# Output-projection products between the units of a dilated attention stage, and two expert weight loads held behind a gather

## The reference

```
proj = rmsnorm(x) @ w_in                      # 4992 columns, split among three head groups
mix  = [hgrn readout (384) | differential attention readout (384) | dilated attention (256)]
h    = x + mix @ w_out                        # 1024 x 1024
u    = rmsnorm(h);  logits = u @ router       # 4 groups, 16 experts; top group, top 2 inside
h    = h + sum over experts of gate * (silu(u @ wg) * (u @ wu)) @ wd
y    = norm(h + sigmoid(rmsnorm(h) @ w_gate) * (p @ w_proj))
```

## Time and profile before

| | |
|---|---|
| three runs | 1004.59, 1002.18, 995.37 us; median 1002.18 |
| profiled execution, first to last instruction | 1003.8 us |
| PE busy | 911.3 us, 91% |
| DVE, ACT, POOL busy | 381.7, 238.8, 82.6 us |
| mean granted TensorE clock | 0.948 of full |
| bytes through DMA | 209.55 MB, mean 209 GB/s |

### The profile page before, as it was taken

The page is one execution under the profiler, slowest core; times in us unless marked ns, Lnnn a source line. Parts: engine busy times, 40 slices in busy tenths (PEclk is TensorE's granted clock), DMA queues, the critical chain, the costliest instruction groups (busy, mean ns, idle before and its releaser), DMA issues.

```text
span 1003.8 us, 15625 instructions
## 1 busy us (share of the span) xinstructions
PE 911.3 (91%) x6377; PEld 483.7 (48%) x6377; DVE 381.7 (38%) x804; ACT 238.8 (24%) x600; POOL 82.6 (8%) x96
## 2 busy tenths in 40 slices
PE   6996999999999999979878993899999898898996
PEld 4453555655456876655445552344344343243442
DVE  5107455564226666454553126311121111111463
ACT  4125222220223323453313111100001000003344
POOL 1000000000024443000000000100000000002100
PEclk9998999999999999967889996899999999999998
DMA  6836133035347753244603707799999999995111
GB/s 220 309 152 178 34 147 147 1 147 183 147 138 235 240 176 109 74 162 144 196 22 122 293 23 281 290 371 372 405 395 383 392 397 410 402 338 187 44 42 44
DMA packets 71186, 209.55 MB, mean 209 GB/s; under 512 B 19113, under 2 KB 51332, under 8 KB 62540
## 3 DMA queue, kind: packets, MB, share of 16 engines
q1 hardware_dynamic: 56432, 185.53, 50.3%
q0 software_dynamic: 3936, 14.22, 4.3%
q10 hardware_dynamic: 10748, 8.80, 2.8%
HBM read 189.09 MB, written 38.26 MB: 226 GB/s over the span
## 4 chain that ended last, share of the span: by engine, by line
PE 78%; DMA 9%; DVE 7%; ACT 4%; issue 2%; SPq 0%; ACTq 0%; DVEq 0%; POOLq 0%
PE ps L2015 17%; PE ps L2427 10%; PE ps L2020 10%; PE ps L2320 6%; PE ps L2550 6%; PE ps L2464 5%; DMA EXPERT<-in_moe_w_up 4%; DMA aF<-in_moe_w_up 2%; PE ps L2052 2%; PE ps L2389 2%; PE ps L2423 2%; PE ps L2098 2%; PE ps L2179 2%; PE ps L2026 1%; PE ps L2125 1%
## 5 line engine op out<-in xcount | busy, mean ns | idle before, releaser
L2015 PE MATMUL ps<-xT,EXPERT 128*128 128x512 f32 x384 | 175.8, 603 | 0.5 <-DVE xT L1310 0.5
L2020 PE MATMUL ps<-EXPERT,xT 128*128 128x384 f32 (+1 forms) x384 | 119.0, 451 | 1.6 <-ACT EXPERT L974 1.6
L2015 PEld LDWEIGHTS ps<-xT,EXPERT 128*128 128x128 f32 x384 | 70.1, 192 | 75.3 <-issue 72.4
L2020 PEld LDWEIGHTS ps<-EXPERT,xT 128*128 128x128 f32 x384 | 77.5, 236 | 23.6 <-issue 1.8
L1917 DVE TENSOR_TENSOR dF<-dF,ps 64x512 f32<-64x512 f32 (+1 forms) x24 | 14.4, 601 | 163.5 <-ACT dF L1206 163.5
L2427 PE MATMUL ps<-EXPERT,wk 128*32 128x512 f32 x448 | 55.6, 642 | 7.8 <-DMA EXPERT<-in_moe_w_up 7.3
L2320 PE MATMUL ps<-EXPERT,xT 128*128 128x512 f32 x128 | 57.2, 597 | 1.1 <-ACT xT L1142 1.1
L2427 PE MATMUL ps<-EXPERT,samp 128*32 128x512 f32 x384 | 57.8, 594 | 0.0
L2550 PE MATMUL ps<-EXPERT 128*128 128x512 f32 x128 | 56.0, 594 | 1.3 <-DVE EXPERT L1970 1.3
L1210 ACT ACTIVATE dF<-ps 128x256 f32<-128x256 f32 (+1 forms) x24 | 8.4, 348 | 166.4 <-PE ps L2447 163.6
L1488 DVE TENSOR_REDUCE small<-ps 128x2 f32<-128x256 f32 (+3 forms) x24 | 19.8, 824 | 63.9 <-PE ps L2101 63.9
(11 more groups left out here) (472 smaller groups left out, 1319.2 us busy)
## 6 DMA issues: line engine op xcount, KB each, us to landing
EXPERT<-in_moe_w_gate SPq DMA_DIRECT2D x12, 2048.0 KB, 17.9
EXPERT<-in_moe_w_up SPq DMA_DIRECT2D x12, 2048.0 KB, 14.5
EXPERT<-in_moe_w_down SPq DMA_DIRECT2D x12, 2048.0 KB, 19.4
EXPERT<-in_w_in SPq DMA_DIRECT2D x13, 1536.0 KB, 6.7
out_win_sample<-in_cache_win SPq DMA_DIRECT2D x16, 1022.0 KB
aF<-in_cache_k_diff SPq DMA_DIRECT2D x32, 192.0 KB, 2.5
aF<-in_cache_v_diff SPq DMA_DIRECT2D x32, 192.0 KB, 2.5
Yd<-wk ACTq DMA_DIRECT2D x34, 128.0 KB
```

What stands on the lines that cost most here:

```text
L2015: last = t.matmul(ps[:, u % 2, :], W_[:, c, c0:c0 + w], xT[:, c, 0:SEQ], start=(c == 0), stop=(c == DC - 1))
L2020: last = t.matmul(ps[:, u % 2, 0:w], rows_, W_[:, c, c0:c0 + w], start=(c == 0), stop=(c == DC - 1))
```

## The change

**Order and gate.** Slab 3 is projected before slabs 10 and 12. The gate's activation and gain and the readout of tile 0 (now in three steps, `roa` on DVE, `roe` on ACT, `rob` on DVE) stand between the last differential units.

**Dilated stage.** `dilated_steps` writes the whole stage out by hand: for unit k it issues `c_s(k)`, `c_t(k-1)`, the steps of `first[k]`, `c_pv(k-1)`, the steps of `second[k]`. Scores have one pair of banks (2 and 3), so `c_s(n)` waits for the exponentials of unit n - 1. Banks 4 and 5 go in turns (`bank_turns`, semaphores `filled` and `taken`) to the transposes of a tile's 768 readout columns (`mtp`, copied to `mixT` by ACT), to the products with row blocks 0 to 5 (`wop`, which DVE adds to the reloaded rows of `XM`), and, once a tile's dilated columns are merged into `mixD`, to their transposes (`mtd`, into `dcols`) and the products with blocks 6 and 7 (`wof`). The sample rows keep one product (`wos`). Root mean square, unit rows, columns and logits of the tiles stand at the end of the list, in the order tile 0, 1, 2, sample, 3. The last `krows` and the routing's constants (`constants`) move between the units too.

**Queues.** SP loads `w_out` in three parts, reloads each tile's input rows right after `mtp` (between the `cached` loads), and writes the values of the differential attention earlier. The expert weights of step 1 now also wait for the last `c_pv`; those of step 0 for the last `wof`; the first two blocks of step 2 wait for the landing of the first gather. The stores to `u2d` move from SP's queue to POOL's, behind its own constants and ahead of its gathers.

```
-ORDER = (0, 1, 2, 4, 5, 6, 7, 9, 11, 8, 10, 12, 3)
+ORDER = (0, 1, 2, 4, 5, 6, 7, 9, 11, 8, 3, 10, 12)
...
+        if u == last[units[u][1]] and c1 == DC and at == NSLAB - 2:
+            steps.append(("w_out_load", 1))
...
+    gated = [("gate_fn",), ("gate_mul",), ("roa", 0), ("roe", 0), ("rob", 0)]
+    at_gate = None
...
+        if at_gate is None and (not todo or todo[0][0] > max(last[3], summed[3])):
+            at_gate = k
+        if at_gate is not None and gated and k >= at_gate:
+            steps.append(gated.pop(0))
+            at_gate = k + GATE_LAG
...
+    steps += gated + [("w_out_load", 0), ("outputs",)]
...
+def dilated_steps():
+    first = {
+        0: mixed_columns(0),
+        1: [("wop", 0, 0, 0), ("wop", 0, 0, 1), ("roa", 1)],
+        2: [("wop", 0, 1, 0), ("wop", 0, 1, 1)],
+        3: mixed_columns(1) + [("roa", 2)],
+        4: [("wop", 1, 0, 1), ("wop", 1, 1, 0)],
+        5: [("wop", 1, 1, 1)],
+        6: [("wop", 2, 0, 0), ("wop", 2, 0, 1), ("roa", 3)],
+        7: [("wop", 2, 1, 0), ("wop", 2, 1, 1)],
+        8: mixed_columns(3) + [("w_out_load", 2)],
+        9: [("wop", 3, 0, 1), ("wop", 3, 1, 0)],
+        10: [("wop", 3, 1, 1)],
+        11: [("mtd", 0)],
+        12: [("wof", 0, 0), ("wof", 0, 1)],
+        13: [("mtd", 1), ("rms", 0)],
+        14: [("wof", 1, 1)],
+        15: [("mtd", 2), ("rms", 1)],
+        16: [("col", 0), ("wof", 2, 1)],
+    }
+    second = {
+        0: [("dec_soft",), ("krows", 0)],
+        1: [("dec_norm",), ("krows", 1), ("krows", 2), ("roe", 1)],
+        2: [("rob", 1), ("krows", 3), ("dec_wt",)],
+        3: values(0) + [("roe", 2), ("wop", 1, 0, 0)],
+        4: values(1) + [("rob", 2)],
+        5: mixed_columns(2) + values(2),
+        6: values(3) + [("roe", 3)],
+        7: values(4) + [("rob", 3)],
+        8: values(5) + [("wop", 3, 0, 0)],
+        9: values(6),
+        10: values(7),
+        11: [("dec_out",)],
+        12: [("roa", NT), ("krows", KR_EARLY), ("roe", NT)],
+        13: [("rob", NT), ("wof", 1, 0), ("krows", KR_EARLY + 1), ("krows", KR_EARLY + 2)],
+        14: [("krows", KR_EARLY + 3), ("krows", KR_EARLY + 4), ("mt",), ("reload", NT), ("constants",)],
+        15: [("wof", 2, 0)],
+        16: [("wos",), ("log", 0), ("rms", 2), ("urow", 0), ("mtd", 3), ("col", 1), ("wof", 3, 0), ("log", 1), ("wof", 3, 1),
+             ("rms", 3), ("urow", 1), ("col", 2), ("log", 2), ("urow", 2), ("col", 3), ("rms", 4), ("log", 3), ("col", 4),
+             ("urow", 3), ("urow", 4), ("log", 4)],
+    }
+    steps = []
+    n_units = 4 * NT
+    for k in range(n_units + 1):
+        if k < n_units:
+            steps.append(("c_s", k))
+        if k:
+            steps.append(("c_t", k - 1))
+        steps += first[k]
+        if k:
+            steps.append(("c_pv", k - 1))
+        steps += second[k]
+    return steps
...
+            def reload(i):
+                src = a["x_prompt"][0, i * P:(i + 1) * P, :] if i < NT else a["x_sample"].rearrange("b t d -> (b t) d")
+                if i < NT:
+                    sp.wait_ge(filled[5], after(("mtp", i, 1)))
+                else:
+                    sp.wait_ge(S_["samp_pe"], 1)
+                sp.dma_start(XM[0:tile_rows(i), i, :], src).then_inc(xload[i], 16)
...
+            sp.wait_ge(S_["c_o_pe"], NCU)
             for kind in range(3):
                 load(1, kind, 1)
-            for p, i in enumerate(SEQ_T):
-                sp.wait_ge(S_["u_ok"], p + 1)
-                sp.dma_start(u2d[i * P:i * P + tile_rows(i), :], Urow[p][0:tile_rows(i), :]).then_inc(S_["u_st"], 16)
-            sp.wait_ge(S_["wo_pe"], WO_ALL)
+            sp.wait_ge(S_["samp_pe"], 2)
+            sp.wait_ge(filled[4], after(("wof", NT - 1, 1)))
             for kind in range(3):
                 load(0, kind, 0)
+            sp.wait_ge(xgload[0], 16)
             load(2, 0, 2)
             sp.wait_ge(S_["rl_pe"], T5)
             load(2, 1, 2)
...
+            for p, i in enumerate(SEQ_T):
+                pool.wait_ge(S_["u_ok"], p + 1)
+                pool.dma_start(u2d[i * P:i * P + tile_rows(i), :], Urow[p][0:tile_rows(i), :]).then_inc(S_["u_st"], 16)
...
+            def wop(i, h, piece):
+                if piece == 0:
+                    return
+                bank, k = TURN["wop", i, h]
+                own = XM[:, i, h * 512:(h + 1) * 512]
+                dve.wait_ge(xload[i], 32)
+                dve.wait_ge(filled[bank], k + 1)
+                v.tensor_tensor(own, own, ps[:, bank, :], ALU.add).then_inc(taken[bank], 1)
...
                 if n == 0:
                     pe.wait_ge(S_["unit_ok"], max(LASTU[12], SUMU[12]) + 1)
                     pe.wait_ge(S_["d_exp"], NT * HB)
-                elif n >= 2:
-                    pe.wait_ge(S_["c_exp"], n - 1)
+                else:
+                    pe.wait_ge(S_["c_exp"], n)
...
+            def mtp(i, part):
+                bank, k = TURN["mtp", i, part]
                 pe.wait_ge(S_["ro_ok"], i + 1)
...
+            def wop(i, h, piece):
+                bank, k = TURN["wop", i, h]
+                if piece == 0:
+                    pe.wait_ge(taken[bank], k)
+                    for part in range(2):
+                        pe.wait_ge(taken[4 + part], after(("mtp", i, part)))
+                if i == 0 and h == 0 and piece == 0:
+                    pe.wait_ge(S_["woload"], 32)
+                for c in ((3, 4, 5), (0, 1, 2))[piece]:
+                    last = t.matmul(ps[:, bank, :], mixT[i % 2][:, c], wout_[c][:, h * 512:(h + 1) * 512],
+                                    start=(c == 3), stop=(c == 2))
+                if piece == 1:
+                    last.then_inc(filled[bank], 1)
...
+            def mtd(x):
+                bank, k = TURN["mtd", x]
+                pe.wait_ge(S_["c_o_ok"], x + 1)
+                pe.wait_ge(taken[bank], k)
```

More of the change, by code:

```diff
@@ L214, in schedule @@
     owed = 0
+    steps.append(("values_out",))
     for k, st in enumerate(d):
@@ L257, in schedule @@
[L257 to L266 removed]
+    steps += gated + [("w_out_load", 0), ("outputs",)]
+    return steps + dilated_steps()
@@ new lines, in mixed_columns, with values @@
+def mixed_columns(i):
+    return [("mtp", i, 0), ("mtp", i, 1), ("reload", i)]
+def values(*bs):
+    out = []
+    for b in bs:
+        out += [("dec_v", 2 * b), ("dec_v", 2 * b + 1)]
+        if b + 2 < NS:
+            out.append(("cached", b + 2, 1))
+    return out
+def dilated_steps():
[51 more added lines that the diff above has]
+    return steps
@@ new lines, in bank_turns @@
+def bank_turns(steps):
+    turn, used = {}, {4: 0, 5: 0}
+    for step, *arg in steps:
+        key, bank = (step, *arg), None
+        if step == "mtp":
+            bank = 4 + arg[1]
+        elif step == "mtd":
+            bank = 4
+        elif step == "wof":
+            bank = 5 - arg[1]
+        elif step == "wop" and arg[2] == 0:
+            key, bank = (step, arg[0], arg[1]), 5 - arg[1]
+        if bank:
+            turn[key] = bank, used[bank]
+            used[bank] += 1
+    return turn
@@ L427, in hybrid_kernel @@
         kvload = [sem(f"kvload{k}") for k in range(2)]
+        filled = {b: sem(f"filled{b}") for b in (4, 5)}
+        taken = {b: sem(f"taken{b}") for b in (4, 5)}
         wload = [sem(f"wload{k}") for k in range(SLOTS)]
@@ L2287, in _ @@
-            does = dict(proj=proj, samp_t=samp_t, lev_mm=lev_mm, kt=kt, h_out=h_out, h_state=h_state, d_s=d_s,
-                        d_t=d_t, d_pv=d_pv, c_s=c_s, c_t=c_t, c_pv=c_pv, krows=krows, dec_soft=dec_soft,
-                        dec_wt=dec_wt, dst_o=dst_o, dec_v=dec_v, dec_out=dec_out, mt=mt)
-            for step, *arg in STEPS:
-                if step in does:
-                    does[step](*arg)
-            def rows_to_columns(src, r, bank):
-                for c in range(DC):
-                    last = t.transpose(ps[:, bank + c // 4, (c % 4) * P:(c % 4) * P + r], src[0:r, c * P:(c + 1) * P],
-                                       ident[0:r, 0:r])
-                return last
```

477 lines of the change are left out of this document (223 added, 254 removed).

## The result

The changed kernel takes 994.36 us (median of 20 executions, 988.24 to 999.34) against 1002.1 us for the kernel before in the same comparison: ratio 0.9921, 95% interval 0.9900 to 0.9943. It is 8 us faster where I had forecast 20. Its profiled execution took 998.44 us with a span of 996.5, 4 us above its median. Every ratio here is to executions of the kernel before made beside it and leaves out those in a slower state (one of a2's six, for one), which the medians keep.

What follows compares the result with a forecast made beforehand. The dilated stage was taken as bound by ACT's and DVE's answers, not PE. 421.4 + 147.8 + 23.8 put the last logits at 593.0, 18.2 earlier; -18.2 - 2.5 + 1 = -19.7 gave 982 us, range 965 to 998.

Steps and rivals of the forecast that it cites:

- The clock rival: Units 12 to 15: some 15 us of PE work run at 1.2 instead of 2.4 GHz, 15 us added, 997; chance 0.10.
- PE's work at full clock: First scores to last logits: PE's remaining work, priced at full clock, sums to 147.8 us.
- The waits: Dilated stage in the new order: PE still waits 23.8 us in all, 9.5 of them after the decode output.
- the slower rival: Dilated units: products stand in series with the waits and the single score tile adds 26 us, 1026; chance 0.05.
- the 6 us for starts: Dilated stage: a wait's own start at each turn, 0.4 us for 16 units, 6 us, bounds 0 and 12.
- Before the stage: Differential units: gate activation and tile 0's readout cost 0, hidden by PE's projections; 4.4 us if a unit waits for all.
- Stores on GpSimd: Five row stores moved to POOL cost 0, landing before the gather's issue; +3 us if the last lands in 12.0.
- the rival's place: Last row store on POOL holds the gather; issue and landing need 18 us instead of 9: +9, 991; chance 0.06.
- The gather: First gather beside expert weights: taken as 7 us, between 4.9 and 9.45, a change of -2.5 us.
- The held blocks: Third expert step's first two weight blocks start at the gather's landing: +1 us for crowding, bounds 0 and 10.4.
- the signs I named for right: Logits near 593, landing near 609, PE over 18 at clock 1.00, ACT-ended waits before `c_pv`, gather 5 to 9 us.
- those for wrong: PE idle before `c_s`; clock 0.5 in 535 to 565; store-released gather over 10 us after logits; down block over 16 us.

Runs made afterwards that it cites:

- a2: Changed kernel with the sample rows' readout and the routing constants on VectorE put behind the next unit's maximum: 987.32 us, 0.9822 of the kernel before.
- e1: Changed kernel with unread identity products, sized a little under PE's waits, ahead of the values of units 10, 11, 12, 14 and tile 3's mixed columns: 991.41 us, 0.9886.
- a3: Changed kernel with the five unit row stores issued by ScalarE on its queue instead of by GpSimd: 997.29 us, 0.9957 of the kernel before.
- d1: Changed kernel with the first step's third weight block also issued only when the first gather has landed: 993.05 us, 0.9927 of the kernel before.
- c2: Changed kernel with tile 0's readout, the sample rows' readout and the routing constants moved later, and the first step's third weight block held: 985.59 us, 0.9839.
- f1: As c2, with the second step's third weight block also held until the first gather has landed: 991.06 us, 0.9904 of the kernel before.
- a4: Changed kernel without the hold, the third step's first two weight blocks issued behind the first step's again: 1002.16 us, 0.9979 of the kernel before.
- b1: Kernel before the change with only the hold added, the third step's first two weight blocks waiting for the first gather's landing: 1004.59 us, 1.0018.
- g1: Changed kernel with the five row stores back on SyncE in front of the first step's weights, and no hold: 998.03 us, 0.9970 of the kernel before.
- b2: Changed kernel with unread identity products ahead of five PE waits, some 21 us of added work for 12.8 us of waits: 1003.45 us, 1.0019.
- c5: Changed kernel with tile 0's readout behind the differential units, and sample rows' readout and routing constants behind the next unit's maximum: 988.58 us, 0.9857.

## Why the prediction was off

The sign held and 994.4 lies inside the range of 965 to 998, but the size was 8 us instead of 20. The clock rival's 997 comes nearest, in part by luck: it had the cause of one of three misses, and in four units only. By steps, in the profiled pair:

- **PE's work at full clock, 147.8 us: the step that failed.** I priced the whole stage at 2.4 GHz and left the lower level to a rival of 0.10 that put it into units 12 to 15 alone. The cheapest prices add up to 134.7, so the list was 13.1 us too dear (bands take fewer keys than the unit I priced, a decode pair 1.74 instead of 1.96). And 21.3 us of work above those prices were missing, most of it at the lower level behind waits from 452 to the end, not in one place. Net of the 1.6 us of waits that I had too many, the stage is 178.3 instead of 171.6. e1 shows the cause for some 6 to 8 us of this rest: the same waits, filled, bring the work behind them back to full speed. For the other slow places, at 452 and in the tail, no run filled the waits. The trace of before had it in view: 0.83 and 0.57 in the earlier trace rows, and 27.4 us by the same balance.
- **The waits, 23.8 us: right.** 22.2 measured (the terms as listed add up to 23.3). None stood ahead of `c_s`, so the slower rival is out. Behind `dec_out` 1.78, 3.40 and 4.04 for 1.5, 3.5 and 4.5; not seen was the 2.49 ahead of unit 10's values. The keys took 2.70 and 1.18 for 2.1 and 0.9, `mt` 1.31 for 1.3, the tail 2.5 for 3.5; the 6 us for starts were mostly not there. a2 shows that VectorE's order makes two of them.
- **Before the stage, 0 (bound 4.4): wrong in the profile, +6.6.** The cover was there for ACT and for the sum of VectorE's work, but not for the instant: 2.1 us of readout put a weighting with two operands in SBUF level with GpSimd's product. The Trainium skill, "SBUF — State Buffer", section "SBUF: two separate sides", says that VectorE and GpSimd share one pair of ports as a lock, taken by whichever starts first for its whole instruction. The trace agrees, 3.95 us against 0.75 by a start 0.43 us later. That the meeting fell on the slow side in this profile is luck; in four of nine it did not. I had read that section for the descriptors of the store and not for this.
- **Stores on GpSimd, 0 (bound +3): +3.0**, and the rival's place was right, its price of 9 us too high. The lock on descriptors, of the same section of the Trainium skill, shows no sign here: ScalarE's queue lands the store later still (a3), and less weight in front of it lands it sooner on the same queue (d1, c2, f1).
- **The gather, -2.5: -5.3 in the profile**, because behind a late store, with the third step's blocks held, it finds the DMA partly idle: a share of 0.20 to 0.70 from 619 to 622, against 0.97 in the earlier trace rows. Without the hold it took 11.1 (a4). By the figures of the Trainium skill, "DMA: Bandwidth & Descriptors", section "Anatomy of one DMA", the estimate was 2.9 us; the 4.12 measured are nearer to that than to my 7.
- **The held blocks, +1: 0.** But their worth was not in my sum at all as what it is. I counted the hold as part of the gather's 2.5 us; a4 makes it 5.8 us by the ratios in this kernel and b1 nothing in the old one.

The forecast's 19.7 us less 6.6 (differential units), 6.7 (stage) and 3.0 (store), plus 2.8 (gather) and 1.0 (blocks) gives the 7.3 of the profiled pair, within rounding.

Not settled: what the row blocks bring by themselves in the median (0 to 6.7 us by g1). Its profile has the last logits end 9.8 us earlier than before, but the profiled execution of before lies above its median: its span alone, 1003.8, is above the median time of 1002.1. How often VectorE comes second, and where the clock falls, in the unprofiled executions isn't known either.

Of the signs I named for right, PE over 18 us of 20 from 440 to 520 (18.35 to 19.64) and waits ahead of `c_pv` ended by ACT's copy were seen. The clock of 1.00 (0.91 and 0.74 in two of those windows), the last logits near 593 (606.2), the landing near 609 (622.6) and a gather between 5 and 9 us (4.12) were not. Of those for wrong, the gather released by a store more than 10 us after the last logits (12.3) was seen. The low clock between 535 and 565 was seen in part (0.83 in 530 to 540 and in 550 to 560, 1.00 between). The third step's down block came 16.2 us after the landing, just over the 16 I had named, but 15.9 before the change, so it tells nothing.

## What to carry to other kernels

Price work at the clock that the stage will be granted. In after, waits of 2.49, 3.40 and 4.04 us on PE cost 1.9, 1.8 and 3.1 us more in the work behind them; the shortened ones of 1.67 in a2 cost nothing there, and one of 1.36 cost nothing in seven profiles and some 5 us in after. So shorten the long waits (here by putting VectorE's long blocks behind the next maximum) before filling PE with work from elsewhere, and don't trust one profile for the short ones. An earlier weight load and a hold in front of a small, urgent transfer are one change: each alone showed no worth here. Before moving VectorE work next to GpSimd work, look at the start times, not at the busy shares.

## What the runs showed of the hardware

- A start 0.02 us behind GpSimd's product made a VectorE instruction of 0.75 us last 3.95; 0.41 us ahead of it, it was not slowed. GpSimd's product took 3.42 us when it was first and 3.64 to 3.92 when VectorE was. The same code fell on the slow side in five and on the other in four profiles, each of another kernel.
- A store of 512 KB from ScalarE's queue let the gather go 17.5 us after its issue, from GpSimd's queue 14.3, both beside weight loads. The Trainium skill, "DMA: Bandwidth & Descriptors", section "Issuing engines are not separate DMA queues", says that a DMA ends up on the same 16 engines whoever starts it; these two runs agree in that the other queue gained nothing. Why it was 3 us later is not shown.
- In b2 the granted clock was 0.58 between 560 and 580 us although PE was busy for 18.69 of the 20, with dummy products for 12.9 of them. I can't say from these runs what they lacked.
- The same wait of 1.36 us on PE was followed by work at half the clock in four profiles and by work at full clock in seven. Behind the wait of 4.04 to 4.06 us it was half in all six that had it; behind those of 1.67 us (two each in a2, c2, c5 and f1) it was full in all.
